# A mixture-of-experts loop: another order of work on ScalarE and VectorE, weights split and awaited in pieces, the place weight multiplied into the silu step

## The reference

```python
def swiglu(x, w_gate, w_up, w_down):
    return (jax.nn.silu(x @ w_gate) * (x @ w_up)) @ w_down
...
    def expert_block(args):
        e, tok_b, wt_b = args
        xb = h_pad[tok_b]
        return swiglu(xb, w_gate[e], w_up[e], w_down[e]) * wt_b[:, None].astype(h.dtype)
    yb = lax.map(expert_block, (block_e, tok.reshape(n_blocks, DISPATCH_BLOCK), wt.reshape(n_blocks, DISPATCH_BLOCK)))
    return jnp.zeros((n + 1, d), h.dtype).at[tok].add(yb.reshape(-1, d))[:n]
```

## Time and profile before

| | |
|---|---|
| three runs, us | 2753.51, 2759.14, 2787.28 |
| median, us | 2759.14 |
| span of the profiled execution, us | 2766.9 |
| first gate matmul of the first block, us from the span's start | 1658.60 |
| first gate matmul of the 97th block, us from the span's start | 2689.59 |
| TensorE busy, share of the span | 89% |
| VectorE, ScalarE, GpSimd busy, share of the span | 45%, 35%, 15% |
| weight loads and row moves between 1658 and 2690 us | 196.09 MB and 69.74 MB |

### The profile page before, as it was taken

The page is one execution under the profiler, slowest core; times in us unless marked ns, Lnnn a source line. Parts: engine busy times, 40 slices in busy tenths (PEclk is TensorE's granted clock), DMA queues, the critical chain, the costliest instruction groups (busy, mean ns, idle before and its releaser), DMA issues. The chain is left out here.

```text
span 2766.9 us, 40539 instructions
## 1 busy us (share of the span) xinstructions
PE 2474.3 (89%) x12053; PEld 1849.0 (67%) x12054; DVE 1238.3 (45%) x2077; ACT 964.8 (35%) x1711; POOL 413.5 (15%) x529
## 2 busy tenths in 40 slices
PE   7999799899998999999978759999988999999890
PEld 1344365599997998985546427777767777777670
DVE  1322146533321111111356757757676655566755
ACT  1211245511100101100220016666676655565652
POOL 0000000000000000000002322333333333333330
PEclk9999859999999999999989769999999999999995
DMA  8410000111101111114140039989999877788964
GB/s 316 186 36 1 6 1 1 46 47 45 38 8 49 41 40 30 45 38 156 61 148 1 0 103 313 283 242 278 273 322 302 250 206 229 202 237 235 299 166 162
DMA packets 263567, 376.50 MB, mean 136 GB/s; under 512 B 18800, under 2 KB 209976, under 8 KB 263512
## 3 DMA queue, kind: packets, MB, share of 16 engines
q1 hardware_dynamic: 233768, 298.73, 32.1%
q0 software_dynamic: 29600, 76.34, 12.0%
q10 hardware_dynamic: 148, 0.75, 0.1%
HBM read 342.52 MB, written 64.82 MB: 147 GB/s over the span
## 5 line engine op out<-in xcount | busy, mean ns | idle before, releaser
L1667 PE MATMUL ex_pgu<-ex_wgu_hi,ex_xT_hi 128*128 (+1 forms) x776 | 319.5, 412 | 59.7 <-DVE ex_xT_lo L1781 53.2
L1776 DVE TENSOR_TENSOR ex_wgu_lo<-ex_stage,ex_wgu_hi (+1 forms) x256 | 296.4, 1220 | 46.9 <-ACT ex_wgu_hi L1726 43.9
L1667 PE MATMUL ex_pgu<-ex_wgu_lo,ex_xT_hi 128*128 (+1 forms) x776 | 310.0, 399 | 0.0
L1667 PE MATMUL ex_pgu<-ex_wgu_hi,ex_xT_lo 128*128 (+1 forms) x776 | 309.5, 399 | 0.0
L1726 ACT CAST ex_wgu_hi<-ex_stage (+1 forms) x256 | 249.5, 1051 | 4.7 <-issue 4.6
L1667 PEld LDWEIGHTS ex_pgu<-ex_wgu_hi,ex_xT_hi 128*128 128x128 f32 x776 | 147.6, 190 | 106.3 <-issue 74.7
L1434 POOL TENSOR_TENSOR sh_s<-sh_s,sh_g 128x544 f32<-128x544 f32 x4 | 5.8, 1453 | 1398.4 <-ACT sh_g L1420 1398.4
L1737 ACT ACTIVATE ex_y<-ex_py,ex_place_weights 128x512 f32<-128x512 f32 x194 | 122.9, 685 | 239.8 <-POOL ex_place_weights L1627 235.9
L464 PE MATMUL qk_pp<-early_late,hT 128*128 128x512 f32 (+1 forms) x432 | 193.0, 600 | 3.6 <-PEq L241 3.6
L1631 POOL DMA_INDIRECT sum_rows<-ex_y,ex_index_scatter x97 | 157.8, 1627 | 212.7 <-ACT ex_y L1737 202.9
L1776 DVE TENSOR_TENSOR ex_wdn_lo<-ex_stage,ex_wdn_hi 128x1024 f32 (+1 forms) x128 | 151.1, 1222 | 64.8 <-ACT ex_wdn_hi L1726 64.8
(11 more groups left out here) (266 smaller groups left out, 4214.4 us busy)
## 6 DMA issues: line engine op xcount, KB each, us to landing
ex_stage<-in_w_exp_gate SPq DMA_DIRECT2D x64, 1024.0 KB
ex_stage<-in_w_exp_up SPq DMA_DIRECT2D x64, 1024.0 KB, 9.3
ex_stage<-in_w_exp_down SPq DMA_DIRECT2D x64, 1024.0 KB, 7.4
w_ada_buf<-in_w_ada SPq DMA_DIRECT2D x5, 4096.0 KB, 15.8
cv_wb<-in_w_in SPq DMA_DIRECT2D x24, 512.0 KB, 3.8
mg_gate_wb<-in_w_in SPq DMA_DIRECT2D x16, 512.0 KB, 4.0
early_late<-in_w_in SPq DMA_DIRECT2D x3, 2048.0 KB, 20.0
n_x<-in_x_prompt POOLq DMA_DIRECT2D x8, 512.0 KB, 7.0
```

The costliest lines, as they stand in the source:

```text
L1667: last = pe.matmul(pgu[:, :], xT[a][:, k, :], w, start=(k == 0 and (a, c) == PASSES[0]), stop=(k == KT - 1 and (a, c) == PASSES[-1]))
L1776: dve.tensor_tensor(dst, src, hi.bitcast(F32), ALU.subtract).then_inc(w_lo, 1)
```

## The change

In the expert loop:

- On ScalarE and VectorE the split of the next expert's gate and up moves from the head of the round to behind `columns`, and the split is that of the expert wanted a block later: it is asked for by `blk_split` of block i+2 instead of i+1. The split of down stays at the round's end, asked for by block i+1. Both engines so read the table twice a round.
- The split of gate and up goes over four pieces of two k steps each, gate and up together, and has its own semaphores (`gu_hi`, `gu_lo`; down: `dn_hi`, `dn_lo`). `gates` waits for piece q ahead of k step 2q, and for each half of the rows ahead of the k steps that use it; `downs` waits for each column half of down.
- Weights are loaded as "(p k) n": partition p holds rows 8p to 8p+7 of gate and up (8 KB in one run), and rows 2p and 2p+1 of down. To match, the transposes of the rows read `xr` with a step of 8 elements (32 bytes), and those of the hidden rows read with a step of 2 elements (8 bytes).
- The stage tile of down has two slots too; SP waits for one `gu_lo` and one `dn_lo` value a round.
- The place weight is a scalar operand of the first silu product (`scalar_tensor_tensor`), the second product is written over `s_` (the tile `h` is gone), ScalarE's `y_out` is a plain copy, and GpSimd's copy of `wcol` is a bare increment of `y_free`.

In every stage: semaphores are allocated for the stage alone, SP clears those of the stage before at the head of the next one (132 clears over the program, 9 to 25 at the head of a stage), and a few are kept for the whole program (`kept_sem`). The tile of the routing scores is freed ahead of the experts.

The core of the diff:

```diff
+    def clear_old(self, sp):
+
+        for s in self.ended:
+            sp.sem_clear(s)
...
-                        sp.dma_start(stage[p][:, bass.ds(slot, 1), :].rearrange("p s (k n) -> p (s k) n", k=k),
-                                     srcs[p][bass.ds(e, 1)].rearrange("e (k p) n -> p (e k) n", p=P)).then_inc(w_loaded[p], 16)
+                        src = srcs[p][bass.ds(e, 1)].rearrange("e (p k) n -> p (e k n)", p=P)
...
+                        sp.dma_start(dst, src).then_inc(w_loaded[p], 16)
...
-                        pool.tensor_copy(wcol[:, :], place_w[:, bass.ds(b, 1)]).then_inc(y_free, 1)
                         pool.tensor_copy(ixy[:, :], place_x[:, bass.ds(b, 1)]).then_inc(idx, 1)
+                        pool.sem_inc(y_free, 1)
...
-                                last = pe.transpose(pt[r][:, k, :], xr[:, (4 * r + k) * P:(4 * r + k + 1) * P], self.ident)
+                                last = pe.transpose(pt[r][:, k, :], xr_k[:, 4 * r + k, :], self.ident)
...
-                        pe.wait_ge(x_lo, b * 2 + 2)
-                        pe.wait_ge(w_lo, ordinal * 6 + (4 + AHEAD))
                         for k in range(KT):
+                            if k % 4 == 0:
+                                pe.wait_ge(x_lo, b * 2 + (k // 4 + 1))
+                            if k % 2 == 0:
+                                pe.wait_ge(gu_lo, ordinal * 4 + (k // 2 + 1))
...
-                            act.activation(y[:, j, :], py[j][:, :], ACT.Copy, scale=wcol[:, 0:1]).then_inc(y_ready, 1)
+                            act.copy(y[:, j, :], py[j][:, :]).then_inc(y_ready, 1)
...
                     with act.Fori(0, n - 1) as i:
-                        following = table(act, self.blk_split, i + 1, NE - 1)
-                        slot = following % 2
-
-                        with act.If(following >= 1):
-                            split(following, slot, (0, 1))
                         sigmoid(i + 1)
                         columns(i + 2)
+                        later = table(act, self.blk_split, i + 2, NE - 1)
+                        with act.If(later >= 1):
+                            split_gu(later, later % 2)
                         y_out(i)
                         hiddens(i + 1)
+                        following = table(act, self.blk_split, i + 1, NE - 1)
                         with act.If(following >= 1):
-                            split(following, slot, (2,))
+                            split_dn(following, following % 2)
...
-                        dve.tensor_tensor(s_[:, :], s_[:, :], pgu[:, 0:DE], ALU.mult).then_inc(silu_done, 1)
+                        dve.scalar_tensor_tensor(s_[:, :], s_[:, :], place_w[:, bass.ds(b, 1)], pgu[:, 0:DE],
+                                                 ALU.mult, ALU.mult).then_inc(silu_done, 1)
...
-                        dve.tensor_tensor(h[:, :], s_[:, :], pgu[:, DE:2 * DE], ALU.mult).then_inc(hidden, 1)
+                        dve.tensor_tensor(s_[:, :], s_[:, :], pgu[:, DE:2 * DE], ALU.mult).then_inc(hidden, 1)
...
-                        with dve.If(following >= 1):
-                            split(following, slot, (0, 1))
                         silu(i + 1)
                         columns(i + 2)
+                        later = table(dve, self.blk_split, i + 2, NE - 1)
+                        with dve.If(later >= 1):
+                            split_gu(later, later % 2)
                         hiddens(i + 1)
```

More of the change, by code:

```diff
@@ L187, in build @@
             self.qkv()
+            self.end_stage()
             self.attention()
+            self.end_stage()
             self.free("V2", "kT", "qT")
@@ L1537, in experts @@
             PIECE = KT * DE
-            stage = [sb(f"ex_stage{i}", [P, 2 if i < 2 else 1, PIECE]) for i in range(3)]
+            stage_gu = sb("ex_stage_gu", [P, 2, 2 * PIECE])
+            stage_dn = sb("ex_stage_dn", [P, 2, PIECE])
             wgu = [sb(f"ex_wgu_{n}", [P, 2, KT, 2 * DE], F32R) for n in ("hi", "lo")]
@@ L1720, in _, with split_gu, split_dn @@
                     n = blocks_of(act)
-                    def split(ordinal, slot, which):
-                        for p in which:
-                            act.wait_ge(w_loaded[p], ordinal * 16 + 16)
-                            for dst, src in halves(0, slot, p):
-                                act.copy(dst, src).then_inc(w_hi, 1)
+                    def split_gu(ordinal, slot):
+                        act.wait_ge(w_loaded[0], ordinal * 16 + 16)
+                        act.wait_ge(w_loaded[1], ordinal * 16 + 16)
+                        for q in range(NQ4):
+                            act.copy(gu_piece(0, slot, q), gu_raw(slot, q)).then_inc(gu_hi, 1)
+                    def split_dn(ordinal, slot):
+                        act.wait_ge(w_loaded[2], ordinal * 16 + 16)
+                        for j in range(2):
+                            act.copy(dn_piece(0, slot, j), dn_raw(slot, j)).then_inc(dn_hi, 1)
                     def columns(b):
```

142 lines of the change are left out of this document (91 added, 51 removed).

## The result

The changed kernel is slower by about 1%: 2797.9 us (median of four runs, 2789.1 to 2803.4) against 2763.9 us of the kernel before in the same series (median of four runs, 2753.5 to 2787.3); the ratio is 1.0107 with a 95% interval of 1.0064 to 1.0149. The prediction was 2705 us, with a range of 2655 to 2768.

What follows compares the result with a forecast made beforehand. TensorE's 9.52 us a round was the floor, with 117 us of waits above it in the expert loop. Loop gains of 62.3 us, less 6.9 for clears and 0.7 for an early split, gave 2705 us, range 2655 to 2768.

Steps and rivals of the forecast that it cites:

- What bounds the kernel: Expert loop: TensorE's floor is 9.52 us a round; 117 us are its waits, 53.2 of them gates awaiting VectorE's rows.
- a lone one: Expert loop, sign of the forecast: a splitting round standing alone should take 9.5 to 9.7 us.
- Order of work: Expert loop: silu and columns ahead of the pieces remove the gates' wait of about 1 us; splitting rounds in a row take 10.0.
- rival C: Expert loop: the gather replaces DVE as the limit, through denser 8-KB runs or later y_out and scatter; 2744 us, chance 0.13.
- A fifth of 0.78: Second half of the expert loop: 0.17 us a round added for splitting rounds that follow each other, giving 9.95.
- Longer runs: Weight loads of the expert loop: 380 GB/s in place of 335, one expert 8.28 us of the engines in place of 9.39.
- Strided reads: TensorE's transposes of rows, read with a 32-byte step: no cost taken; four times as long would cost 1.08 us a round.
- rival D: TensorE's transposes: strided loads take four times as long, making the kernel slower than before, 2782 us; chance 0.10.
- Small edits: Expert loop: place weight in silu costs 5% of 0.41 us, taken as nothing; copies on ScalarE and GpSimd lie off the path.
- The clears: Stage heads on SP: 99 of 132 stand ahead of an awaited load, 0.07 us each, 6.9 us; under 2 us per head.
- within 2% of before: Whole kernel: chance 0.52 that the time is neither under 2704 us (0.44) nor over 2814 us (0.04).

Runs made afterwards that it cites:

- e12: Changed kernel with weight runs of 1 KB (down 4 KB), loading only half of each weight matrix in the loop: loop 968.6 us, ratio 0.9729 to the kernel before.
- e11: Kernel before, loading only the first half of each weight matrix's runs in the loop: loop 1021.3 us, ratio 0.9940.
- e16: Changed kernel with its 8-KB runs, y_out and hiddens moved between the second and third of the four gate and up pieces: 2744.4 us, ratio 0.9917 to the kernel before.
- e3: Kernel before with weights loaded in runs of 8 KB and the strided transposes: loop 1035.2 us, ratio 0.9976.
- e6: Kernel before with the semaphore clears at stage heads and the score tile freed, expert loop as before: loop 1037.7 us, ratio 1.0001.

## Why the prediction was wrong

**What bounds the kernel** was read rightly in the main. Of the 117 us that I called waits, 85.1 stand in the trace as TensorE's idle time. That the old order costs time is shown by e12 against e11, with half of the loads. The gates' wait fell to 20.4 us in the changed kernel (I had said under 10), and 26 splitting rounds take 9.5 to 9.7 us, as forecast for a lone one; the rounds behind them do not.

**Order of work** is the step that failed. I saw that `y_out` would stand behind the four hi pieces, up to 4 us later, but gave this no term in the sum: its scatter was "ahead of the next gather in GpSimd's queue only one round on", and what it could do went into rival C. The loop lost 36 us where I had it gain 62, and e16, in which only `y_out` and `hiddens` move up between the pieces, goes from 1.0107 to 0.9917. I followed DVE's chain to its end (10.0 us) and did not follow ScalarE's in the same way: `y_out`, the scatter, its landing, then the next `y_out`, and `hiddens` and downs behind that. Nor did I ask what SP issues at the moment at which the scatter goes out: both hang on the fourth piece of one split. For a table load and its branch I had taken 0.23 us; ahead of the hi pieces ScalarE stands idle for 0.85 us in the round shown (2229.27). (A fifth of 0.78, the step in the second half's sum, is 0.16 and not 0.17, 0.7 us of the 62.)

**Longer runs**: the term was right in size (380 GB/s forecast, 381 measured; 513 us of the engines where before had 585) and its effect on the time had the wrong sign. I counted the weights' own time and not what a packet of 8 KB does to the other queue: about 28 us between 1 and 8 KB in the changed order (loops of 1038.7 and 1067.1 us, ratios of 1.0005 and 1.0107), nothing in the old order (e3). That the wait for the gather rises with the packets is measured (21.6, 24.8, 41.8 and 58.8 us in the loop for 1, 2, 4 and 8 KB); that the turns of the two queues are the reason is read from the stretches above.

**Strided reads** cost nothing, as taken (1.04 against 1.03 us for eight transposes); rival D fell, and the penalty at 16-byte lines that the prediction cites from the Trainium skill (page "SBUF — State Buffer", section "Door 1: The DMA port swizzle (why `[64,N]` ≈ `[32,N]`)") does not show in these transposes.

**Small edits**: a silu step with the place weight took 0.48 us (2236.97) in place of 0.41, more than the 5% taken; no run has this edit alone. The clears: SP's first load stands 3.5 us behind the start of the experts' stage (1621.92 to 1625.39) in place of 2.2 (1636.16 to 1638.31), so under 2 us, as forecast; e6 shows no loss that can be told, so the 6.9 us for all of them are neither borne out nor refuted.

**The rivals**: C held in kind. Rows waited 59 us for the gather where I had said over 40 would show it. Its price (2744) was 54 us too low: it had the landing of the gather alone, and what the late `y_out` does in ScalarE's stream was missing; and the sum left no slack for any transfer that lands later than before. The range ended at 2768 and so did not hold the time. That the time would be within 2% of before was given 0.52 and came true, by luck: those chances were spread around a gain.

## What to carry to other kernels

When a long piece of work is moved within an in-order stream, follow what now stands behind it up to the transfers that it releases, and see which other transfers are released at the same moment: in the rounds shown here 2 us decided whether a scatter went ahead of 2 MB of loads or among them. A larger DMA run was cheaper for its own queue and, where another queue was at work at the same time, dearer for that one, so its price is read together with the transfers beside it. Halving a load shows quickly whether an order is good and merely starved, or bad in itself. And a loop is compared by its idle time as well as by its length, since TensorE's busy time in one and the same kernel differed by 16 us between two profiles.

## What the runs showed of the hardware

Two queues that both had work got one packet each: 50 packets of 4 KB against 49 of 8 KB in 2 us, 88 of 4 KB against 87 of 1 KB. Reading a row tile with a step of 32 bytes for transposes went at the pace of a contiguous one: 1.04 against 1.03 us for eight transposes. In attention, in which TensorE (PE) was busy for 8.0 of the first 18.5 us, its clock rose from 1.2 to 2.4 GHz at a point that varied between executions of one and the same kernel: the mean granted clock from 350 to 410 us was 0.53 in one and 0.87 in the other, and the stage took 199 and 180 us. In the expert loop of the same two executions the granted clock was 0.99 and 0.98, and TensorE's busy time 945.9 and 961.8 us.
